# Stick-breaking attention: scores kept on VectorE, logarithms in two rounded parts, 0/1 products in one-pass matmuls

## The reference

```
z        = q k^T * scale                                    (512 x 512 per head)
strict   = s < t
log_keep = where(strict, log_sigmoid(-z), 0)
later    = reverse cumsum of log_keep over s, without s itself
a        = where(strict, exp(log_sigmoid(z) + later), 0)
y        = a v
```

## Time and profile before

| | |
|---|---|
| median of 3 runs | 3535.99 us (3534.68 to 3544.18) |
| the profiled execution: its span | 3547.3 us (no other time of it is recorded) |
| TensorE busy | 3342.8 us, 94% |
| VectorE busy | 1721.0 us, 49% |
| ScalarE busy | 1314.1 us, 37% |
| GpSimd busy | 1066.8 us, 30% |

### The profile page before, as it was taken

The page is one execution under the profiler, slowest core; times in us unless marked ns, Lnnn a source line. Parts: engine busy times, 40 slices in busy tenths (PEclk is TensorE's granted clock), DMA queues, the critical chain, the costliest instruction groups (busy, mean ns, idle before and its releaser), DMA issues.

```text
span 3547.3 us, 45185 instructions
## 1 busy us (share of the span) xinstructions
PE 3342.8 (94%) x17356; PEld 2676.9 (75%) x17356; DVE 1721.0 (49%) x3168; ACT 1314.1 (37%) x2278; POOL 1066.8 (30%) x517
## 2 busy tenths in 40 slices
PE   8999999999999899999899889999999988889999
PEld 6677787777867778777787578888888656668887
DVE  5347335433237633542688766222465655543234
ACT  4333324333333332333433443222343455533232
POOL 3123122234303222114335622322453100034443
PEclk9999999999999999999999899999999999999999
DMA  5532121133552122113222001121232110022232
GB/s 181 183 132 79 45 79 54 63 100 104 178 195 98 48 67 84 45 60 123 82 72 78 1 20 58 60 72 60 99 128 79 45 44 1 1 66 94 95 101 78
DMA packets 88344, 288.53 MB, mean 81 GB/s; under 512 B 10048, under 2 KB 20672, under 8 KB 87360
## 3 DMA queue, kind: packets, MB, share of 16 engines
q1 hardware_dynamic: 86832, 274.77, 22.9%
q10 hardware_dynamic: 1296, 10.87, 0.8%
HBM read 281.40 MB, written 4.19 MB: 81 GB/s over the span
## 4 chain that ended last, share of the span: by engine, by line
PE 54%; DVE 7%; ACT 2%; issue 2%; POOL 0%; DVEq 0%; ACTq 0%; POOLq 0%
PE psum L308 14%; PE psum L309 14%; PE psum L310 14%; PE psum L307 9%; PE psum L3718 1%; DVE mla_cols L3807 1%; PE psum L3706 1%; PE psum L1182 1%; DVE h_low L572 0%; PE psum L3684 0%; DVE padded L2756 0%; DVE ml_weights L3159 0%; DVE squares L501 0%; ACT mla_probs L3763 0%; ACT weights_high L385 0%
## 5 line engine op out<-in xcount | busy, mean ns | idle before, releaser
L403 POOL TENSOR_TENSOR weights_low<-weights_loaded,weights_high 128x1024 fp32r<-128x1024 f32 (+3 forms) x460 | 969.3, 2107 | 2394.3 <-ACT weights_high L385 2307.5
L308 PE MATMUL psum<-h_high,weights_high 128*128 128x512 f32 (+1 forms) x2400 | 907.4, 378 | 45.6 <-DVE h_low L572 21.1
L309 PE MATMUL psum<-h_low,weights_high 128*128 128x512 f32 (+1 forms) x2400 | 888.8, 370 | 0.0
L310 PE MATMUL psum<-h_high,weights_low 128*128 128x512 f32 (+1 forms) x2400 | 887.9, 370 | 0.0
L385 ACT CAST weights_high<-weights_loaded 128x1024 fp32r<-128x1024 f32 (+3 forms) x460 | 425.3, 924 | 476.9 <-PE psum L310 400.3
L308 PEld LDWEIGHTS psum<-h_high,weights_high 128*128 128x128 f32 x2400 | 458.8, 191 | 134.3 <-issue 35.7
L309 PEld LDWEIGHTS psum<-h_low,weights_high 128*128 128x128 f32 x2400 | 459.1, 191 | 78.0 <-issue 4.1
L310 PEld LDWEIGHTS psum<-h_high,weights_low 128*128 128x128 f32 x2400 | 457.6, 191 | 77.2
L308 PE MATMUL psum<-act_high,weights_high 128*128 128x512 f32 (+1 forms) x528 | 187.8, 356 | 8.2 <-DVE act_low L4105 6.2
L310 PE MATMUL psum<-act_high,weights_low 128*128 128x512 f32 (+1 forms) x528 | 187.6, 355 | 0.0
L309 PE MATMUL psum<-act_low,weights_high 128*128 128x512 f32 (+1 forms) x528 | 187.6, 355 | 0.0
(11 more groups left out here) (497 smaller groups left out, 5376.7 us busy)
## 6 DMA issues: line engine op xcount, KB each, us to landing
weights_loaded<-stream_dram SPq DMA_DIRECT2D x472, 512.0 KB, 3.3
weights_loaded<-stream_dram SPq DMA_DIRECT2D x80, 128.0 KB, 2.4
weights_loaded<-stream_dram SPq DMA_DIRECT2D x24, 384.0 KB, 3.0
weights_loaded<-stream_dram SPq DMA_DIRECT2D x8, 272.0 KB, 5.5
x<-x_dram SPq DMA_DIRECT2D x4, 512.0 KB, 6.7
arena_mem<-mem_dram ACTq DMA_DIRECT2D x2, 1024.0 KB, 4.9
x<-x_dram ACTq DMA_DIRECT2D x1, 2048.0 KB, 8.9
x_kept_dram<-x ACTq DMA_DIRECT2D x1, 2048.0 KB, 9.3
```

Of the source, the lines that this page charges most:

```text
L308: pe.matmul(out, a.high, b.high, start=start, stop=False)
L309: pe.matmul(out, a.high, b.low, start=False, stop=False)
L310: return pe.matmul(out, a.low, b.high, start=False, stop=stop)
L403: pool.tensor_tensor(self.low[s][:, 0:size], raw[:, 0:size], self.high[s][:, 0:size], ALU.subtract).then_inc(*g.event("weights_low").up(po ...
```

## The change

TensorE's `weights` no longer computes z a second time and no longer adds the mask. VectorE keeps the negated scores with the mask in them (`neg`), and after the suffix sums it subtracts `neg` from the bank into `wt` (new function `scored`, between `kept` of the next head and the two fills). ScalarE takes the exponential of `wt` in SBUF. log_keep goes to TensorE in two rounded parts: ScalarE copies `wt` to `keep.high` (new function `rounded`, after `logs`), VectorE writes `keep.low` = `wt` - `keep.high`. The 0/1 matrices are copied to rounded tiles once a layer, so that each sum takes two one-pass products in place of one f32 product. In `kept` the subtraction for block b-1 is issued after the first operation of block b. The constant `before01` goes away. The new tiles lie in the room of `x` (which is kept in DRAM during the branches) and of `merged`, as views only; the hunks that lay them out are left out below.

```diff
@@ -1652,7 +1652,7 @@
         if j == 0:
             fill_tensor(g)
     values_tensor(g, key("v"), turn, COL["sb_v"], (l,), h)
-    ready = [S("zeroed").at("queries"), S("drained").at(key("v"))]
+    ready = [S("zeroed").at("queries"), S("sums_rounded").at(l), S("drained").at(key("v"))]
     ready += [S("drained").at(key(n, j)) for n in "qk" for j in range(2)]
 
     def scores(hd):
@@ -1665,23 +1665,24 @@
                True).then_inc(*S("scored").up(pe, key(hd, b)))
 
     def weights(hd):
-        j, lk = hd // 2, t.lk[hd % 2]
+        keep = t.keep[hd % 2]
         for b in range(QT):
             n = SEQ - b * P
             bank = g.banks(g.claim(key("w", hd, b), turn.next(1)))
-            mm(g, bank[:, 0:n], t.k[:, j, b * P:(b + 1) * P], t.q[:, hd, b * P:SEQ], True, False)
-            mm(g, bank[:, 0:P], g.ident, g.c.before_add, False, False)
             for m in g.after(pe, S("kept").at((l, hd))):
                 pe.wait_ge(*m)
-            done = mm(g, bank[:, 0:n], g.c.from_here, lk[b], False, b == QT - 1)
+            mm(g, bank[:, 0:n], g.c.from_here_rounded, keep[b].high, True, False)
+            done = mm(g, bank[:, 0:n], g.c.from_here_rounded, keep[b].low, False, b == QT - 1)
             for b2 in range(b + 1, QT):
-                done = mm(g, bank[:, (b2 - b) * P:n], g.ones, lk[b2], False, b2 == QT - 1)
+                own = bank[:, (b2 - b) * P:n]
+                mm(g, own, g.c.ones_rounded, keep[b2].high, False, False)
+                done = mm(g, own, g.c.ones_rounded, keep[b2].low, False, b2 == QT - 1)
             done.then_inc(*S("scored").up(pe, key("w", hd, b)))
 
     def weigh(hd):
         wt = t.wt[hd % 2]
         i = g.claim(key("o", hd), turn.next(1))
-        for m in g.after(pe, S("drained").at(key("w", hd, QT - 1))):
+        for m in g.after(pe, S("stick_weight").at((l, hd))):
             pe.wait_ge(*m)
         for q in range(QT):
             for b in range(q + 1):
@@ -1703,6 +1704,10 @@
 def sb_scalar(g, l, opening):
     act, S, t = g.act, g.event, g.t.sb
     key = lambda *a: ("sb", l) + a
+    for rounded, exact in ((g.c.from_here_rounded, g.c.from_here), (g.c.ones_rounded, g.ones)):
+        for m in g.after(act, S("first_in").at(0)):
+            act.wait_ge(*m)
+        act.copy(rounded, exact).then_inc(*S("sums_rounded").up(act, l))
     for j in range(2):
         g.weights.round(key("q", j))
         pair_scalar(g, key("q", j), pair_of(t.q, j), SCALE)
@@ -1723,19 +1728,27 @@
                 act.wait_ge(*m)
             act.activation(wt[b], wt[b], ACT.Ln, bias=1.0).then_inc(*S("stick_log").up(act, (l, hd, b)))
 
+    def rounded(hd):
+        wt, keep = t.wt[hd % 2], t.keep[hd % 2]
+        for b in range(QT):
+            for m in g.after(act, S("stick_kept").at((l, hd, b))):
+                act.wait_ge(*m)
+            act.copy(keep[b].high, wt[b]).then_inc(*S("kept_high").up(act, (l, hd, b)))
+
     def weights(hd):
         wt = t.wt[hd % 2]
         for b in range(QT):
-            k = key("w", hd, b)
-            for m in g.after(act, S("scored").at(k), S("kept").at((l, hd))):
+            for m in g.after(act, S("drained").at(key("w", hd, b))):
                 act.wait_ge(*m)
-            act.activation(wt[b], g.bank(k)[:, 0:SEQ - b * P], ACT.Exp).then_inc(*S("drained").up(act, k))
+            act.activation(wt[b], wt[b], ACT.Exp).then_inc(*S("stick_weight").up(act, (l, hd) if b == QT - 1 else None))
 
     logs(0)
+    rounded(0)
     fill_scalar(g)
     for hd in range(HEADS):
         if hd + 1 < HEADS:
             logs(hd + 1)
+            rounded(hd + 1)
         fill_scalar(g)
         weights(hd)
         fill_scalar(g)
@@ -1750,30 +1763,43 @@
             fill_vector(g)
 
     def negated(hd):
-        lk, wt = t.lk[hd % 2], t.wt[hd % 2]
+        neg, wt = t.neg[hd % 2], t.wt[hd % 2]
         before = [S("weighed").at(key(hd - 2))] if hd > 1 else []
         for b in range(QT):
             k = key("z", hd, b)
             for m in g.after(dve, S("scored").at(key(hd, b)), *before):
                 dve.wait_ge(*m)
-            dve.tensor_scalar(lk[b], g.bank(k)[:, 0:SEQ - b * P], -1.0, None, ALU.mult).then_inc(
+            dve.tensor_scalar(neg[b], g.bank(k)[:, 0:SEQ - b * P], -1.0, None, ALU.mult).then_inc(
                 *S("drained").up(dve, k))
             for m in g.after(dve):
                 dve.wait_ge(*m)
-            dve.scalar_tensor_tensor(wt[b], lk[b], -1.0, lk[b], ALU.mult, ALU.min).then_inc(
-                *S("stick").up(dve, (l, hd, b)))
-
-    def kept(hd):
-        lk, wt = t.lk[hd % 2], t.wt[hd % 2]
-        for b in range(QT):
-            for m in g.after(dve, S("stick_log").at((l, hd, b))):
-                dve.wait_ge(*m)
-            dve.scalar_tensor_tensor(lk[b], lk[b], 0.0, wt[b], ALU.min, ALU.subtract).then_inc(
-                *S("stick").up(dve))
+            dve.tensor_tensor(neg[b][:, 0:P], neg[b][:, 0:P], g.c.before_add, ALU.subtract).then_inc(*S("stick").up(dve))
             for m in g.after(dve):
                 dve.wait_ge(*m)
-            dve.tensor_tensor(lk[b][:, 0:P], lk[b][:, 0:P], g.c.before01, ALU.mult).then_inc(
-                *S("kept").up(dve, (l, hd) if b == QT - 1 else None))
+            dve.scalar_tensor_tensor(wt[b], neg[b], -1.0, neg[b], ALU.mult, ALU.min).then_inc(
+                *S("stick").up(dve, (l, hd, b)))
+
+    def kept(hd):
+        neg, wt, keep = t.neg[hd % 2], t.wt[hd % 2], t.keep[hd % 2]
+        for b in range(QT + 1):
+            if b < QT:
+                for m in g.after(dve, S("stick_log").at((l, hd, b))):
+                    dve.wait_ge(*m)
+                dve.scalar_tensor_tensor(wt[b], neg[b], 0.0, wt[b], ALU.min, ALU.subtract).then_inc(
+                    *S("stick_kept").up(dve, (l, hd, b)))
+            if b:
+                for m in g.after(dve, S("kept_high").at((l, hd, b - 1))):
+                    dve.wait_ge(*m)
+                dve.tensor_tensor(keep[b - 1].low, wt[b - 1], keep[b - 1].high, ALU.subtract).then_inc(
+                    *S("kept").up(dve, (l, hd) if b == QT else None))
+
+    def scored(hd):
+        neg, wt = t.neg[hd % 2], t.wt[hd % 2]
+        for b in range(QT):
+            k = key("w", hd, b)
+            for m in g.after(dve, S("scored").at(k)):
+                dve.wait_ge(*m)
+            dve.tensor_tensor(wt[b], g.bank(k)[:, 0:SEQ - b * P], neg[b], ALU.subtract).then_inc(*S("drained").up(dve, k))
 
     def gated(hd):
         k = key("o", hd)
@@ -1790,6 +1816,7 @@
         if hd + 1 < HEADS:
             negated(hd + 1)
             kept(hd + 1)
+        scored(hd)
         fill_vector(g, 2)
         gated(hd)
 
```

More of the change, by code:

```diff
@@ L4279, in pack_constants @@
     at["causal"] = first.const(causal)
-    at["before01"] = first.const((i < j) * 1.0)
     at["before_add"] = first.const(np.where(i < j, 0.0, NEG))
@@ L4375, in name_constants @@
     sq = lambda t, n: t[:, at[n]:at[n] + P]
-    c.before01, c.before_add, c.from_here = (sq(first, n) for n in ("before01", "before_add", "from_here"))
+    c.before_add, c.from_here = (sq(first, n) for n in ("before_add", "from_here"))
     c.perm64, c.perm32 = sq(first, "perm64"), sq(first, "perm32")
@@ L4420, in layout_first @@
     with ExitStack() as s1:
+        with ExitStack() as s2:
+            sb("keep_apart", [P, 5 * BANK], s2)
+            t.keep_merged = sb("keep_merged", [P, 3 * BANK], s2, F32R)
         t.merged = sb("merged", [P, KT, SEQ], s1)
@@ L4452, in layout_first @@
     heads = [("k", [P, 2, SEQ]), ("v", [P, QT, BR])]
-    pieces = [(f"{n}{b}", [P, SEQ - b * P]) for n in ("lk", "wt") for b in range(QT)]
+    pieces = [(f"{n}{b}", [P, SEQ - b * P]) for n in ("neg", "wt") for b in range(QT)]
     of = carve(even, heads + pieces)
     sets = (of, carve(t.merged[:, :, :].rearrange("p k n -> p (k n)"), pieces))
-    t.sb = tiles(of, q=t.q_even, lk=[[o[f"lk{b}"] for b in range(QT)] for o in sets], wt=[[o[f"wt{b}"] for b in range(QT)] for o in sets])
+    parts = [carve(tile, [(f"{n}{b}", [P, SEQ - b * P]) for n in names for b in range(QT)] + more)
+             for tile, names, more in ((t.keep_x, ("high0", "low0", "high1"), [("from_here", [P, P]), ("ones", [P, P])]),
+                                       (t.keep_merged, ("low1",), []))]
+    high = [[parts[0][f"high{i}{b}"] for b in range(QT)] for i in range(2)]
+    low = [[parts[i][f"low{i}{b}"] for b in range(QT)] for i in range(2)]
+    t.sb = tiles(of, q=t.q_even, keep=[[Split(*p) for p in zip(*s)] for s in zip(high, low)],
+                 **{n: [[o[f"{n}{b}"] for b in range(QT)] for o in sets] for n in ("neg", "wt")})
     of = carve(odd, heads + [("c_kv", [P, 1, SEQ]), ("c_n", [P, 1, SEQ]), ("qi", [P, SEQ]), ("ki", [P, SEQ]),
@@ L4469, in layout_first @@
                                           ("mem", [P, KT, N_MEM])]), q=t.q_even)
-    return name_constants(at, t_common, t.first)
+    c, s = name_constants(at, t_common, t.first)
+    c.from_here_rounded, c.ones_rounded = parts[0]["from_here"], parts[0]["ones"]
```

(3 more changed lines are left out.)

2 lines of the change are left out of this document (1 added, 1 removed).

## The result

The changed kernel takes 3571.4 us (median of 4 runs, 3567.0 to 3582.8), the kernel before 3540.1 in the same comparison: 1.0079 of it, 95% interval 1.0062 to 1.0096. Slower, as forecast, but by 31 us where I had put 14, and outside the range (3534 to 3563). The change is small, 0.8%; it is called slower because the interval lies clear of 1.

A forecast was written before the change was run, and what follows sets the result against it. TensorE, busy 94%, bounds the kernel before; with the change VectorE's loop binds. Two layers of 0.6 us plus 6.6 us of clock loss give +14.4 on 3536.0: 3550.4 us, range 3534 to 3563.

The forecast's parts named there:

- the stall for ScalarE's copy: In kept, VectorE's low-part subtraction waits for ScalarE's copy of the high part: 0 to 0.6 us a head.
- the loop: VectorE to drain, then TensorE's next adaLN step, value product and scores, back to VectorE: 18.4 us against a head of 17.45.
- Rivals 1 and 2: First: VectorE binds, clock stays up, 3537 us (half loss 3544), chance 0.18. Second: TensorE stays the bound, 3508 us, chance 0.1.
- Rival 4: Suffix sums: rounded passes bring nothing over f32 passes of the same width, 4.3 us; 3553 us, chance 0.04.
- rival 3: ScalarE-VectorE hops or low-part subtraction cost more, e.g. 0.2 us a hand-over, two low-clock windows per stop; 3565 us, chance 0.08.
- The smaller time by 56 ns for 128 columns: Suffix sums at the skill's back-to-back gap: 0.45 us less a head, 0.9 us in all.
- start of the second negated: On VectorE, negated of head 1 starts later, by +2.2 us a layer.
- two loops, without the clock: Two VectorE loops cost 36.8 us instead of the measured 35.7, +1.1 a layer.
- head 2, negated to B: TensorE's second adaLN step in head 2 starts 12.2 us after negated instead of 11.25, +1.0 a layer.
- clock, three stops: TensorE's clock falls behind three waits a layer, 2.2 us of work lost each (1.6 to 2.8), 6.6 us a layer.
- sums of head 3 to the end: Last head: shorter sums count, -4.7 us; the last adaLN step waits for scored, +1.0; a layer.
- the last cast for the next branch still ends under the value product: At the end of each stretch, the cast for the next branch stays hidden under the value product; no cost.

The follow-up runs named there:

- e1: Changed kernel with four extra f32 products of 512 columns per head on TensorE between the suffix sums and the next adaLN step; 1.0070 of the kernel before, 3563.3 us.
- e7: Changed kernel with three f32 products of 512 columns on TensorE right behind the stop in heads 0 to 2; 1.0109 of the kernel before, 3582.2 us.
- e8: Changed kernel with twelve f32 products of 8 columns on TensorE right behind the stop in heads 0 to 2; 1.0186 of the kernel before, 3609.5 us.
- e11: Kernel before with 20 extra VectorE operations a head ahead of the drain in heads 0 to 2; 1.0177 of the kernel before, 3603.9 us.
- e3: Changed kernel with scored ahead of kept of the next head, drains behind negated and kept, exponentials ahead of roundings; 0.9966 of the kernel before, 3528.9 us.
- e4: Changed kernel with f32 suffix sums of the kept scores, no rounding copies or low parts; 1.0018 of the kernel before, 3548.1 us.
- e5: Changed kernel with rounded sums, but second score product and mask kept on TensorE, no scored; 1.0006 of the kernel before, 3545.6 us.
- e6: Kernel before with 12 extra VectorE operations a head ahead of the drain in heads 0 to 2; 1.0054 of the kernel before, 3563.8 us.
- e2: Changed kernel with the drain moved ahead of kept on VectorE and the row copy ahead of the roundings on ScalarE; 1.0027 of the kernel before, 3552.4 us.
- e9: Order of e3, plus the first drain ahead of kept of head 0 and first row copy ahead of its roundings; 0.9997 of the kernel before, 3539.6 us.
- e10: Changed kernel with the edits of e3 and e4 together: reordered, f32 sums without rounding; 0.9953 of the kernel before, 3525.9 us.

## Why the prediction was right in sign and too small in size

Right, with their sizes: VectorE becomes the bound, by scored and the low parts ahead of the drain (12.17 us against 12.15); the stall for ScalarE's copy 0.22 us within 0 to 0.6; scored 2.07 against 2.1; the sums 2.8 us against 2.75; the loop 18.5 in e1 against 18.4; TensorE's saving turned into stops (31.2 us of waits on the drain against "30 us and more"). Rivals 1 and 2 fell with the traces: the clock did not stay up, and TensorE did not stay the bound. Rival 4 fell with the short sums of the kernel after (2.8 us). The time came out beyond rival 3 (3565), whose two conditions fared differently: the hand-overs between the engines are not dearer (0.22 us), but its second low window behind a stop did come, behind three of six. I had given the two together 0.08, and by their own terms (1.2 + 9.6 + 6 x 4.4 us) their time was 3573, not 3565. The smaller time by 56 ns for 128 columns is out as well: with a weight load for each pass they came every 0.11 us (210.17 and 210.28 in the kernel after).

In the two stretches the profiled execution lost 27.7 us where I had 14.4. By the steps of the sum, layer 0 and layer 1:

| step | forecast a layer | layer 0 | layer 1 |
|---|---|---|---|
| start of the second negated | +2.2 | +2.3 | +2.3 |
| two loops, without the clock | +1.1 | +1.4 | +1.4 |
| head 2, negated to B | +1.0 | +1.0 | +0.9 |
| clock, three stops | +6.6 | +12.3 | +9.7 |
| sums of head 3 to the end | -3.7 | -1.6 | -2.0 |

The clock row is the loops above 18.5 us (23.67 and 20.17 in layer 0) and the time from B of head 2 to the sums of head 3, 14.84 us against 9.37 before. The last row is 218.47 - 207.58 against 12.48 before.

**The step that failed is the size of the clock term.** I wrote that the six windows gave "6 x 0.37 = 2.2 us of work lost (1.6 to 2.8)", and carried this to the new stops. Behind those six stops nothing more was lost: in the second 6 us the clock was back at 1.00 behind all six. Three of them in the kernel before:

```profile
890.30:896.30 6.00, 6.00 (x28) 1.00 0.73 259
...
1773.10:1779.10 6.00, 6.00 (x29) 1.00 0.24 87
...
3183.20:3189.20 6.00, 6.00 (x28) 1.00 0.24 87
```

So longer windows would not have helped; the fault was to carry their price to stops with other work behind them. Behind the stops of the kernel after, the second 6 us are at 0.50 three times out of six, and e7 and e8 show that what runs first behind a stop changes how long the clock stays low. In the kernel after the first windows lost 2.6 us on average and the second ones 1.5, together 4.1 a stop, where I had 2.2; the clock row of the table gives 22.0 / 6 = 3.7, and e11 gives 4.7 for stops of much the same length. With 4.1 the sum would have been +26 us.

**The second step that failed was costed at nothing**: "the last cast for the next branch still ends under the value product". It does not; the branch waits 1.42 and 1.23 us for it. The sums of the last head had become 4.7 us shorter, while the load of these weights, issued behind the step that frees its buffer, took no less time than before (6.8 us against 5.7). I had named the cover (2.28 us of value product) without looking at when the cast's own input arrives. The rest of that row's miss, 0.7 and 0.5 us, I did not follow up.

I also overlooked the stop ahead of the first A (4.05 us, for the row copy behind ScalarE's roundings); by VectorE's times it cost nothing on the path, since VectorE's chain ran on as forecast.

What stays open first: why, behind like stops with the same work, the clock came back within 6 us in three cases and only after 12 us in three others.

And the 6 to 7 us by which the profiled execution of the kernel after is longer outside the stretches (790.3 us between them against 784.1). They can be located: 130 to 195 us behind the first stretch, in a part that the change does not touch, the granted clock is 0.83 in the kernel after (348.47 to 413.47) and 0.92 in the kernel before (333.12 to 398.12), which is 6 us of 65. The same part is at 0.92 in e3, e4, e7 and e11, at 0.87 to 0.88 in e5 and e6 and at 0.83 to 0.84 in e1, e2, e8, e9 and e10; e10 has the lowest time of all and 789.4 us between its stretches. One trace a kernel can't say whether this belongs to the kernel or to the one execution, so it is not a price of the change that is shown.

## What to carry to other kernels

A short drain that another engine waits for belongs ahead of every long group of operations, and a consumer of the current head ahead of preparing the next one: the same operations in another order turned +0.8% into -0.3%. Of the change itself only the half that drops the second score product paid, and only in the new order (e10, -0.5%, against e3 with the rounding, -0.3%, intervals overlapping; e5, the rounding alone, no change). Work taken from the bound engine pays only until the next loop binds; add up that loop with the new operations before choosing how much to move. Price a stop of TensorE by a stretch in which the same work follows a stop; the same clock windows behind other work gave half the price here.

## What the runs showed of the hardware

The low level of TensorE's clock lasted through 12 us and more of unbroken work (0.50 over 192.74 to 204.74, behind a stop of 5.46 us), while in e7 a stop of 5.19 us with three 512-column products first was followed by full clock in the second 6 us. With the same work behind it, a stop of about 5 us cost 3.7 to 4.7 us beyond its own length on average; stops of 0.7 to 2.9 us (e6) cost 1.5 on average, from nothing to 12 us at the low level. The Trainium skill, "TensorE: Matmul & The Clock Gate", section on the HAM clock gate, says that the unthrottled clock has to be earned by activity and is lost by idling. The stops agree with the second half. On the first half e7 agrees, but in e8 and behind three stops of the kernel after TensorE was busy throughout and the clock stayed at 0.50 to 0.62 for 12 us: being busy did not suffice, and no run here shows what would.
